# A gather in four quarters: in the last, VectorE adds every second row and TensorE runs 34 more gate units for three token tiles

## The reference, cut to what matters

```python
# first block, last part (per token: 8 heads x 16 picks = 128 rows)
w   = softmax(top16 scores) * gelu(h2 . u[index])
x   = x + sum over picks of w * v[index]
x   = rms_norm(x, final_g)
# second block
h = rms_norm(x, norm_g[l])
p = h @ w_in[l]
(p_r, p_k, p_v, p_w, p_a, z_a, p_q, p_sk, p_sv, z_b, p_xq, z_c, p_gate) = split(p)
y_a = rwkv7_mix(p_r, p_k, p_v, p_w, p_a, ...) * silu(z_a)
y_b = sliding_window_sink_attn(p_q, p_sk, p_sv, ...) * silu(z_b)
y_c = memory_cross_attn(p_xq, mem, ...) * silu(z_c)
gates  = sigmoid(p_gate)
merged = gates[0]*(y_a @ w_a) + gates[1]*(y_b @ w_b) + gates[2]*(y_c @ w_c)
x = x + merged @ w_out
```

## Time and profile before

| what | us |
|---|---|
| median of 3 runs | 2531.84 |
| lowest and highest of them | 2519.61, 2534.78 |
| profiled execution: span of the records | 2514.7 |
| TensorE busy in it | 2232.3 (89%) |
| VectorE busy | 1702.5 (68%) |
| GpSimd busy | 883.5 (35%) |
| ScalarE busy | 862.1 (34%) |

### The profile page before, as it was taken

The page is one execution under the profiler, slowest core; times in us unless marked ns, Lnnn a source line. Parts: engine busy times, 40 slices in busy tenths (PEclk is TensorE's granted clock), DMA queues, the critical chain, the costliest instruction groups (busy, mean ns, idle before and its releaser), DMA issues. The chain is left out here.

```text
span 2514.7 us, 33903 instructions
## 1 busy us (share of the span) xinstructions
PE 2232.3 (89%) x12198; PEld 1425.3 (57%) x12198; DVE 1702.5 (68%) x3859; ACT 862.1 (34%) x1980; POOL 883.5 (35%) x649
## 2 busy tenths in 40 slices
PE   8998999998988998777778887888899899999999
PEld 7886667754444444322333333444468787777787
DVE  7998797577677666677777767776664843646453
ACT  3222763243232333232332224322324222246441
POOL 0001213354544455433344554355522222212243
PEclk9999999999999999999999899999999999989999
DMA  4332215599999999999999999999983221332252
GB/s 150 109 106 96 84 52 205 195 413 414 395 421 418 410 411 419 398 422 421 416 411 410 408 400 408 422 406 415 417 319 127 83 69 68 120 109 89 84 198 100
DMA packets 125685, 692.49 MB, mean 275 GB/s; under 512 B 13392, under 2 KB 13776, under 8 KB 59728
## 3 DMA queue, kind: packets, MB, share of 16 engines
q0 software_dynamic: 73728, 536.90, 52.0%
q1 hardware_dynamic: 51792, 153.43, 17.2%
HBM read 668.79 MB, written 21.50 MB: 275 GB/s over the span
## 5 line engine op out<-in xcount | busy, mean ns | idle before, releaser
L2038 PE MATMUL bank<-peer_uv,peer_diag 128*128 128x512 f32 x2048 | 973.8, 621 | 216.6 <-ACT peer_diag L1440 210.6
L1787 DVE SCALAR_TENSOR_TENSOR peer_uv<-peer_uv,h 128x1024 f32<-128x1024 f32 x512 | 654.5, 1289 | 377.6 <-DMA peer_uv<-in_peer_uv,peer_index 377.4
L1487 POOL DMA_INDIRECT peer_uv<-in_peer_uv,peer_index x512 | 554.0, 1082 | 714.0 <-PE bank L2038 627.7
L2038 PEld LDWEIGHTS bank<-peer_uv,peer_diag 128*128 128x128 f32 x2048 | 389.4, 197 | 703.2 <-issue 699.5
L162 PE MATMUL bank<-hT_high,weight_high 128*128 128x512 f32 (+1 forms) x952 | 427.8, 449 | 14.8 <-POOL weight_low L230 8.1
L230 POOL TENSOR_TENSOR weight_low<-weight_ring,weight_high 128x1024 fp32r<-128x1024 f32 x86 | 210.5, 2448 | 644.4 <-ACT weight_high L213 644.4
L164 PE MATMUL bank<-hT_high,weight_low 128*128 128x512 f32 (+1 forms) x952 | 364.2, 383 | 0.0
L163 PE MATMUL bank<-hT_low,weight_high 128*128 128x512 f32 (+1 forms) x952 | 364.1, 383 | 0.0
L1435 ACT ACTIVATE peer_gelu<-peer_dots 128x2 f32<-128x2 f32 (+1 forms) x257 | 52.2, 203 | 780.4 <-DVE peer_uv L1787 780.0
L213 ACT ACTIVATE weight_high<-weight_ring 128x1024 fp32r<-128x1024 f32 x171 | 180.5, 1056 | 372.4 <-PE bank L164 365.4
L162 PEld LDWEIGHTS bank<-hT_high,weight_high 128*128 128x128 f32 x952 | 180.8, 190 | 81.9 <-issue 41.7
(11 more groups left out here) (458 smaller groups left out, 2777.3 us busy)
## 6 DMA issues: line engine op xcount, KB each, us to landing
weight_ring<-in_weights SPq DMA_DIRECT2D x184, 512.0 KB
z_store<-fill_stage SPq DMA_DIRECT2D x70, 256.0 KB, 2.4
peer_uv<-in_peer_uv,peer_index POOLq DMA_INDIRECT x512, 8.8
merge_z<-z_store SPq DMA_DIRECT2D x8, 768.0 KB, 5.9
merge_z<-z_store SPq DMA_DIRECT2D x12, 512.0 KB, 4.8
raw_query<-in_weights SPq DMA_DIRECT2D x10, 512.0 KB, 6.6
raw_out<-in_weights SPq DMA_DIRECT2D x8, 512.0 KB, 6.1
swz<-z_store SPq DMA_DIRECT2D x1, 2560.0 KB, 10.1
```

What stands on the lines that cost most here:

```text
L1487: pool.indirect_dma_start(uv[:, p % SLOTS], None, peer_uv, bass.IndirectOffsetOnAxis(index[:, n % 2, p % TOPK:p % TOPK + 1], 0)).then_inc( ...
L1787: nc.vector.scalar_tensor_tensor(uv[:, p % SLOTS, 0:D], uv[:, p % SLOTS, 0:D], 1.0, h2[:, t], ALU.mult, ALU.mult, accum_out=dots[:, p % TO ...
L2038: mm = nc.tensor.matmul(bank[2 * t + c][:], diag[:, p % SLOTS], uv[:, p % SLOTS, D + c * 512:D + (c + 1) * 512], start=(n == first_of(t) a ...
```

## The change

Three things change, and the line numbers of the changed file are some 25 to 90 higher.

1. From group 207 to 254 VectorE takes over the odd pick of each group (`by_vector`): it adds weight x row to x of the last tile itself (`add_rows`, one group late), with no diagonal and no TensorE matmul. POOL's gathers then also wait for `vector_added`.
2. `EARLY = 34` units of `fill2` are computed for the first three tiles in the same stretch, behind the 13 rwkv units: 47 units with 376 steps in place of 13 with 104, of which 352 are spread over the 47 groups (7 or 8 a group) and 24 come after the last sum. ACT takes them through `early_stage`, and SP stores them. Their weights are loaded and split for this, and loaded a second time in the second block.
3. In the second block those 34 units need only the last tile: 4 steps of two plain fp32 matmuls of 128 columns, unsplit. The other 12 stay as they were. The dealing is new: levels of `rwkv_core` 3 in place of 7, attn2 2 a round in place of 4, attn3 none in place of 2. The list is now 34 x 4 + 12 x 8 = 232 steps, and the 136 small ones end exactly with the two pairs of `rwkv_core` (78 + 29 + 29).

```diff
+EARLY = 34
-WHOLE = range(first_unit("rwkv3"), first_unit("rwkv3") + 13)
+WHOLE = range(first_unit("rwkv3"), first_unit("rwkv3") + 13 + EARLY)
...
+            if n < self.part:
+                each = DT // PART_STEPS
+                for f in range(each * k, each * (k + 1)):
+                    mm = self.nc.tensor.matmul(to, self.ring[:, f], self.last[:, f], start=f == 0, stop=f == DT - 1)
...
+VECTOR_EVERY = 2
+Z_AFTER = 3
+EARLY_UNITS = Z_UNITS + EARLY
+def early_steps_up_to(g):
+
+    return DT * (EARLY_UNITS - Z_AFTER) * max(g + 1 - Z_FROM, 0) // (Z_UNTIL - Z_FROM)
...
 def z_group(n):
 
-    g = Z_FROM + (DT * (n + 1) - 1) // 2
-    return g if g < Z_UNTIL else LAST_GROUP + 1
+    return next((g for g in range(Z_FROM, Z_UNTIL) if early_steps_up_to(g) >= DT * (n + 1)), LAST_GROUP + 1)
+def by_vector(p):
+
+    return Z_FROM <= p // GROUP < LAST_GROUP and p % VECTOR_EVERY == VECTOR_EVERY - 1
...
-                w.load(sp, r0 + Z_UNITS)
+                w.load(sp, r0 + Z_UNITS + RING)
+                for n in range(EARLY):
+                    sp.wait_ge(z_kept, Z_UNITS + n + 1)
+                    if n == EARLY - RING:
+                        sp.wait_ge(summed, LAST_GROUP - 1)
+                    w.load(sp, r0 + Z_UNITS + RING + n + 1)
+                    sp.dma_start(early_store[n][:, 0:EARLY_T], early_stage[:, n % 2]).then_inc(early_stored[n % 2], 16)
...
-                            QUERIES + DT + 2 <= lows < QUERIES + DT + Z_UNITS and
+                            QUERIES + DT + 2 <= lows < QUERIES + DT + EARLY_UNITS and
                             z_group(lows - QUERIES - DT - 2) + RINGS + 2 <= g):
...
                     if g >= RINGS:
                         pool.wait_ge(summed, g - RINGS + 1)
+                        if vector_picks(GROUP * (g - RINGS + 1)):
+                            pool.wait_ge(vector_added, vector_picks(GROUP * (g - RINGS + 1)))
...
+                def add_rows(g):
+
+                    for p in picks(g):
+                        if by_vector(p):
+                            dve.wait_ge(weight_ready, g + 1)
+                            if vector_picks(p):
+                                dve.wait_ge(vector_added, vector_picks(p))
+                            nc.vector.scalar_tensor_tensor(x[:, TT - 1], uv[:, p % SLOTS, D:2 * D], weight[:, p % TOPK:p % TOPK + 1],
+                                                           x[:, TT - 1], ALU.mult, ALU.add).then_inc(vector_added, 1)
...
-                    if Z_FROM <= g < Z_UNTIL:
-                        next(early, None)
+                    for _ in range(early_steps(g)):
                         next(early, None)
...
-                        fill.pe(pe, 7)
+                        fill.pe(pe, 3)
...
-              out=lambda g: at(y, g), group=8, dim=HD, fill=fill, fill_steps=2, row_scale=(table(0), table(1)),
+              out=lambda g: at(y, g), group=8, dim=HD, fill=fill, fill_steps=1, row_scale=(table(0), table(1)),
...
-              out=lambda g: at(y, g), group=4, dim=P, fill=fill, fill_steps=2, row_scale=(table(2), table(3)),
+              out=lambda g: at(y, g), group=4, dim=P, fill=fill, fill_steps=0, row_scale=(table(2), table(3)),
```

More of the change, by code:

```diff
@@ L258, with __init__ @@
 class Filler:
-    def __init__(self, nc, st, w, banks, unit, items, store):
+    def __init__(self, nc, st, w, banks, unit, items, store, part=0, last=None):
         self.nc, self.w, self.banks, self.unit, self.items, self.store = nc, w, banks, unit, items, store
+        self.part, self.last = part, last
         self.kept = st.sem("kept")
@@ L267, in __init__ @@
         self.stage = st.sb("stage", [P, 2, T])
+        self.begins = [0]
+        for n in range(len(items)):
+            self.begins.append(self.begins[-1] + (PART_STEPS if n < part else DT))
         self.step = self.taken = self.sent = self.early = self.before = 0
@@ L270, in __init__, with done_at, here @@
         self.marks = []
+    def done_at(self, step):
+        return sum(b <= step for b in self.begins[1:])
     @property
     def done(self):
-        return self.step // DT
+        return self.done_at(self.step)
+    def here(self, n):
+        return slice(EARLY_T if n < self.part else 0, T)
     def pe(self, pe, steps):
         self.early = self.done
-        for _ in range(min(steps, DT * self.limit - self.step)):
-            n, k = divmod(self.step, DT)
-            src = self.items[n][0]
+        for _ in range(min(steps, self.begins[-1] - self.step)):
+            n = self.done
+            k = self.step - self.begins[n]
             if k == 0:
-                self.ring = self.w.wait(pe, self.unit(n))
+                self.ring = self.w.wait_whole(pe, self.unit(n)) if n < self.part else self.w.wait(pe, self.unit(n))
                 if n >= len(self.banks):
                     pe.wait_ge(self.kept, n - len(self.banks) + 1)
-            mm = product(self.nc, self.banks[n % len(self.banks)][:], self.ring[:, k], src[:, k], k == 0, k == DT - 1)
-            if k == DT - 1:
+            to = self.banks[n % len(self.banks)][:, self.here(n)]
+            if n < self.part:
+                each = DT // PART_STEPS
+                for f in range(each * k, each * (k + 1)):
+                    mm = self.nc.tensor.matmul(to, self.ring[:, f], self.last[:, f], start=f == 0, stop=f == DT - 1)
+                ends = k == PART_STEPS - 1
+            else:
+                mm = product(self.nc, to, self.ring[:, k], self.items[n][0][:, k], k == 0, k == DT - 1)
+                ends = k == DT - 1
+            if ends:
                 mm.then_inc(self.w.done, 1)
@@ L303, in act @@
         if upto is None:
-            upto = max(self.early, (self.step - 6) // DT)
+            upto = max(self.early, self.done_at(self.step - 6))
         while self.taken < upto:
@@ L319, in sp @@
             sp.wait_ge(self.kept, n + 1)
-            sp.dma_start(self.store[n], self.stage[:, n % 2]).then_inc(self.stored[n % 2], 16)
+            sp.dma_start(self.store[n][:, self.here(n)], self.stage[:, n % 2, self.here(n)]).then_inc(self.stored[n % 2], 16)
             self.sent += 1
@@ L1146, in merge_and_experts @@
         z_kept, last_act, last_dve = (st.sem(n) for n in ("z_kept", "last_act", "last_dve"))
+        early_stored = [st.sem(f"early_stored{i}") for i in range(2)]
+        vector_added = st.sem("vector_added")
         iota = const.whole("iota").rearrange("p (a b) -> p a b", a=TOPK)
@@ L1453, in _ @@
                         next(memories)
-                    if zs < Z_UNITS and z_group(zs) < g:
+                    while zs < EARLY_UNITS - Z_AFTER and z_group(zs) < g:
                         keep_z(zs)
                         zs += 1
-                assert zs == Z_UNITS - Z_AFTER
+                while zs < EARLY_UNITS - Z_AFTER:
+                    keep_z(zs)
+                    zs += 1
                 nc.scalar.activation(warm[:, 1:2], warm[:, 0:1], ACT.Sqrt)
+                keep_z(EARLY_UNITS - 3)
                 next(norming[TT - 1])
                 next(norming[TT - 1])
-                keep_z(Z_UNITS - 2)
+                keep_z(EARLY_UNITS - 2)
                 next(norming[TT - 1])
-                keep_z(Z_UNITS - 1)
+                keep_z(EARLY_UNITS - 1)
                 for _ in norming[TT - 1]:
@@ L1489, in _ @@
                                                 ).then_inc(arrived[g % RINGS] if g < LAST_GROUP else last_arrived[p % GROUP], 16)
-                for n in range(lows, QUERIES + DT + Z_UNITS):
+                for n in range(lows, QUERIES + DT + EARLY_UNITS):
                     w.low_part(pool, nc.gpsimd, u0 + n)
@@ L1852, in early_z @@
                     pe.wait_ge(low_kept, 3 * DT)
-                    for n in range(Z_UNITS):
+                    for n in range(EARLY_UNITS):
                         ring = w.wait(pe, r0 + n)
@@ L2076, in spread, with second_block @@
     return mm
[L2079 removed]
+def second_block(nc, ctx, w, bank, a, x, hT, mem_store, z_store, out, dump, load, places):
     cols_sb = ctx.enter_context(nc.sbuf_tensor("cols2", [P, sum(COLS2.values())], F32))
```

71 lines of the change are left out of this document (50 added, 21 removed).

## The result

The changed kernel takes 2592.02 us (median; 2590.53 to 2597.88) against 2529.14 for the kernel before in the runs of that comparison (2519.61 to 2534.78): a ratio of 1.0263, 95% interval 1.0238 to 1.0288. The forecast was slower, 2574, with a range from 2500 to 2620.

What follows compares the result with a forecast made beforehand. DMA was taken to bound the gather's last quarter, TensorE the second block (VectorE and ScalarE's chain where fills are thin). +140 + 7.5 - 106 = +42 on 2531.84 gave 2574 us, range 2500 to 2620 (its own 2550 to 2600).

Steps and rivals of the forecast that it cites:

- The wait on the low part: Gather's last quarter: in 34 of 47 groups TensorE waits for GpSimd's split behind sum and two gathers, chain 5.0 to 5.4 us.
- The gather's +140: Last quarter: 34 waiting groups of 9.1 us, 13 of 6.2 and some 5 for group 254, 395 in place of 254.
- 3.5 x 0.52 = 1.8: Waiting groups of the last quarter: 3.5 steps behind the wait at 0.52 us each, 1.8 us of a group's 9.1.
- alone wins nothing: Last quarter: VectorE's odd picks take 1.72 us a group off TensorE but gain nothing while DMA bounds.
- The bound of part 2 if DMA decides: Last quarter: 24.5 MB for 34 early units at 2.82 us per MB, 69 us, or 6.8 a group.
- The tail: After the last sum: 24 steps in place of 10, 14 x 0.52 = +7.5 us.
- The second block: Fewer and smaller TensorE fill steps save 106 us over prepare, pairs, attn2, attn3 and merge; bounds -123 and -70.
- attn2's "-20": Second block, attn2: 38 steps of 0.68 us fewer give -20; a round of 4.56 would be 3.2, below that VectorE and ScalarE bound.
- VectorE ended with the split each time: Reading of earlier rows: VectorE's multiplication (2.77 us) and dot product (3.13) beside GpSimd splits ended when the split did.
- The first rival: Last quarter: the split is hidden and DMA stays the bound, groups of 6.8 us, -30 in all, 2502; chance 0.17.
- The third rival: Second block returns only 70 as attention and prepare fall back on VectorE and ScalarE, +78, about 2610; chance 0.15.
- the second: Rival, last quarter: late weights, SP queue or additions lengthen the chain 2 us in 34 groups, +70, about 2640; chance 0.11.

Runs made afterwards that it cites:

- low_earlier: The changed kernel with GpSimd splitting each early unit one iteration earlier (RINGS + 1 in place of RINGS + 2): 2488.09 us, ratio 0.9844 to the kernel before.
- low_last: The changed kernel with each early unit's 16 high-part matmuls first and its 8 low-part ones last, behind the wait: 2486.69 us, ratio 0.9856 to the kernel before.
- keep_warm: The changed kernel with 7 to 22 useless matmuls ahead of each of the 35 early units that wait for their low part: 2557.01 us.
- part1_alone: The changed kernel with EARLY = 0 and the old dealing of fills, so only VectorE's odd picks remain: 2545.5 us, ratio 1.0084 to the kernel before.
- part1_add_first: part1_alone with VectorE's addition of group g-1 moved ahead of its wait for the rows of group g: 2526.27 us, ratio 1.0004 to the kernel before.
- low_vector: low_last with the early units' low parts written by VectorE in place of GpSimd: 2461.72 us, ratio 0.9745 to the kernel before.
- attn2_bare: The changed kernel with no fill steps in attn2's 19 rounds, 38 steps moved to the start of the merge: 2626.23 us, ratio 1.0389 to the kernel before.
- low_vector_fourth: low_vector with VectorE adding every fourth row only (VECTOR_EVERY = 4): 2468.51 us, ratio 0.9757 to the kernel before.
- no_add: The changed kernel with TensorE summing both picks of every group and VectorE adding none: 2645.66 us, ratio 1.0489 to the kernel before.

## Why the prediction was right or wrong

**The wait on the low part: right, in place and price.** 34 groups were counted and 35 came (unit 42 waits for its split too: it stands behind the last gathers). The end of the wait was worked out at 1.87 + 5.4 = 7.27 us from the group's start and was 7.33. `low_earlier` and `low_last` show that it was the cause: 104 and 105 us.

**The gather's +140: too small by 52; the failing step is "3.5 x 0.52 = 1.8"**, the steps behind the wait. They took 3.07: after the wait TensorE's granted clock was at 0.50, and a step took 0.90 us on average in place of 0.52. That is 35 x 1.3 = 45 us, and `keep_warm` takes 43 off the quarter. The forecast carried the clock of a busy TensorE, 0.97 in the earlier trace rows, into a stretch that it had itself just filled with idle time. The other 7 are one more waiting group (9.1 for 6.2: 3), 11 groups without a wait of 6.4 in place of 6.2 (2), and the two ends of the quarter (1).

**Part 1 "alone wins nothing": right that it wins nothing, wrong at zero.** It costs 18 us in the quarter through the held slot (`part1_alone`, `part1_add_first`). In the changed kernel that price is hidden: only 13.3 of the gathers' 232.1 us of idle time there are ended by additions. In it, part 1 gains: without it the kernel is 54 us slower. The bound of part 2 if DMA decides, 69 us for 34 units, was near: `low_vector` has 56.4 (310.96 - 254.61), 1.7 a unit for 2.0.

**The tail: +10.2 for +7.5**, the same 14 steps more, and a longer way from the last of them to the first unit with `last_h`.

**The second block: -124.0 for -106**, 16 of the 18 in four stages. rwkv_prepare gave 16.9 for 17.5, the pairs 40.8 for 38 (levels of 5.5 to 6.4 in the first pair), and attn2 29.5 for 20; attn3 with the fills at the start of the merge 34.5 for 30.5. The step that failed is attn2's "-20". It names a round of 3.2 us, which is what TensorE's 26 us less would leave, with VectorE and ScalarE as the floor below that; but -20 stands for a round of (85.9 - 20)/19 = 3.5. The round became 56.4/19 = 2.97, below both, and `attn2_bare` has 2.7 even at a low clock, so no floor stood at 3.2. Chain and finish_branches, costed at 0, gave 3.7 between them, and the rest of the merge took 1.4 more, both less than the traces tell apart.

**One reading of rows was wrong, without a price.** "VectorE ended with the split each time" does not fit: the dot product ended 1.09 us behind the split and the multiplication 0.55. They did their work after it, so the block is the whole split.

**The net** of +42 against +63 in the medians (+75 between the profiled executions) thus came from two errors of opposite sign, 52 and 18. The forecast's own range, 2550 to 2600, held the time, but by luck in part: with the second block as forecast it would have been some 2610. The first rival (split hidden, 2502) is what `low_earlier` and `low_last` made true by hand, at 2487. The third rival was wrong in sign. Of the second, little was seen in the changed kernel: splits found their high part ready but for 10.3 us of idle time in the quarter, and the 0.38 us a group that part 1 added to the chain is far from its 2.

## What to carry to other kernels

When a change makes a unit of work as short as the period of the loop that feeds it, look at how far ahead of its use each helper step is issued: an order that was two periods early becomes half a period late, and no share of busy time shows it coming. TensorE's waits here cost their own length (3.0 us on average) and then 1.3 us more in the slow steps behind them, so price both. And when a second engine joins in reading a buffer, ask when it reads last in its own program order: the slot is held until then.

## What the runs showed of the hardware

- **The clock after a short wait.** In the group shown, a wait of 2.3 us between stretches of full work was followed by three steps at a granted clock of 0.50; in the next group it was back (0.93 over 1850.03 to 1853.00). Matmuls whose results are thrown away kept it at 0.99 and made the program 35 us faster.
- **GpSimd and VectorE.** In `low_earlier` VectorE's additions took 2655 ns on average beside GpSimd's splits, and in `low_vector` 1278, where VectorE did the splits itself. Gathers suffer too. From `low_earlier`'s timelines of POOL and DVE:

```profile
1764.17 1.65 POOL L1561 DMA_INDIRECT peer_uv<-in_peer_uv,peer_index  x1 [2.25 <-DVE x L1685]
1766.13 0.93 POOL L1561 DMA_INDIRECT peer_uv<-in_peer_uv,peer_index  x1 [0.30 <-issue]
1767.08 2.39 POOL L241 TENSOR_TENSOR weight_low<-weight_ring,weight_high 128x1024 fp32r<-128x1024 f32 x1
```

```profile
1763.79 1.20 DVE L1878 SCALAR_TENSOR_TENSOR peer_uv<-peer_uv,h 128x1024 f32<-128x1024 f32 x1
...
1766.95 3.62 DVE L1685 SCALAR_TENSOR_TENSOR x<-peer_uv,peer_weight,x 128x1024 f32<-128x1024 f32 x1
```

The gather at 1764.17, begun within a dot that ends at 1764.99, takes 1.65 us in place of 0.93. In this quarter 63 gathers began within a dot or an addition and took 1.36 us on average, the other 27 took 0.94. The reverse is not seen. In `low_vector`, where GpSimd has gathers alone, VectorE began 65 two-input instructions, nearly all dots, while a gather was running, and they took 1.22 us, as at other times; five additions that began so in `low_vector_fourth` took 1.26 to 1.28.

The addition at 1766.95 began 0.13 us ahead of the split and still lasted to 1770.57, 1.10 behind the split's end. In `low_earlier` 15 additions that began 0.13 to 0.44 us ahead of a split lasted 3.6 to 3.9 us so; dots and additions that began 0.64 us or more ahead of one took their usual time, and the split took 2.5 to 2.8 us. The Trainium skill ("SBUF — State Buffer", section "Who interferes with whom") has it that a VectorE instruction with two SBUF inputs and a GpSimd instruction that reads SBUF exclude each other, and that whichever was issued first keeps the other out to its end. That one stands aside for the other agrees with these rows. By the recorded starts the first does not always win: the 15 additions disagree, and why is not shown. The 44 us that the prediction worked out from that rule for additions that keep splits out did not come. The chain was 7.33 us long for 7.27 worked out without it, and without any additions (`no_add`) it was only 0.38 us shorter.
